# Attention ahead of the recurrence in both mixers of a two-layer trunk, with the fourth adaptive matrix loaded into other cells

## The chip, the cores and the metric

One NeuronCore of one Trainium2 chip runs the whole program in one launch. The metric is the device time of that launch in microseconds (us). The kernel is written in Bass: each engine (TensorE, VectorE, ScalarE, GpSimd) and each DMA queue has a program of its own that runs strictly in order, and semaphores are all that ties them together. In the profile PE is TensorE, PEld its weight loads, DVE VectorE, ACT ScalarE, POOL GpSimd; SPq is the queue of DMA transfers that SyncE issues, POOLq the one that GpSimd issues.

## What is computed

x is 256 tokens of 1024 channels in float32. Two layers, each a mixer and a channel mixer, each of the two behind its own adaptive modulation: four adaptive matrices in all (1024 rows by 3072 columns, three 1024-column parts: shift, scale, gate), numbered ada 0 to ada 3. The channel mixer of layer 0 is a dense SwiGLU, that of layer 1 routes over eight experts.

```python
def _modulate(c_act, w, b):
    m = (c_act @ w + b)[:, None, :]
    return jnp.split(m, 3, axis=-1)          # shift, scale, gate

def _hybrid_mixer(h, ...):
    c_q, c_kv, k_r, x_rec, g_rec = jnp.split(h @ w_in, IN_SPLITS, axis=-1)
    q = (_rms(c_q) @ w_q_up)                  # 8 heads of 64 + 32 (rope)
    kv = (_rms(c_kv) @ w_kv_up)               # 8 heads of 64 keys + 64 values
    attn = causal_attention(qf, kf, v)        # 2 blocks of 128 queries
    xr = causal_conv(x_rec, conv_w, conv_b)   # 4 taps
    r, i = sigmoid(xr @ w_a + b_a), sigmoid(xr @ w_x + b_x)   # block-diagonal
    log_a = 8 * r * log_sigmoid(lam)
    u = sqrt(-expm1(2 * log_a)) * (i * xr)
    h = scan(a=exp(log_a), u)                 # h[t] = a[t] * h[t-1] + u[t]
    rec = h * gelu(g_rec)
    return concat(_rms(attn), _rms(rec)) @ w_out

for l in range(2):                            # x = residual stream
    x += gate * _hybrid_mixer(_rms(x) * (1 + scale) + shift, ...)   # ada 0, ada 2
    x += gate * (_swiglu if l == 0 else _moe)(modulated _rms(x))    # ada 1, ada 3
```

## The kernel before

**The stages**, by the trace, in us from the start of the span: conditioning, ada 0 and layer 0's input projection (0 to 74); mixer 0 (74 to 162); the dense feed-forward (162 to 361); layer 1's input projection (ending at 406); mixer 1 (to 493); the router (to 507); the eight experts (to 1516). x stays in SBUF.

**Memory.** Weights stream from HBM through numbered cells of an arena (cells 0 to 2 of 3072 columns, 5 and up in the working area, `TOKENS` and 12 in other tensors). `fills` in `trunk()` is a table written out by hand: (what, which, piece, cell, waits). SyncE runs it from top to bottom; an entry with a wait holds all that stand behind it. The queue of layer 1's start is this: the last feed-forward pieces, the four pieces of w_in of layer 1, gate bias 2, ada 3's eight pieces of 128 rows (1.57 MB each), the small weights (q and kv up-projections, the block-diagonal gates), w_out, then the experts. The matrix of ada 2 goes through GpSimd's queue (the table `late`).

**An adaptive matrix** is summed over its 1024 rows by VectorE: `steps("ada", a, ks)` runs L1334 (one multiply by a column of c, piece 0) or L1336 (multiply and add to an accumulator, pieces 1 to 7), 3072 columns each; every piece is thus one step of the counter `ada_step`. TensorE then adds the 128 partitions (`ada_columns`) and VectorE forms the columns of shift and scale (`modulation(a)`, counter `mod`). In layer 1 ada 3's steps run while TensorE does the input projection (L643, L650), whose last column tiles are those of the latents and of the convolution.

**A mixer** (`mixer(l)` in each engine's program, the numbered lines are those of before):

- TensorE: transposes of the normed latents (L675), kv and q up-projections (L693), transposes of q and k per token block (`turn_qk`, L702), the scores of block 0 (L714, L720); then, ahead of the second block, the gate products of the recurrence `gates(0)`; transposes of q and k of block 1, its scores (L742, L745); `gates(1)`; transposes of the first block's probabilities s0 (L755), its outputs (L760), transposes and outputs of the second block's two halves of heads (L767, L776), transposes of the head outputs (L785), and the output projection (L795 in two parts, the attention's rows and then the recurrence's).
- VectorE: latents' scaling (L1522), taps of the convolution (`tap0` comes from ScalarE, taps 1 to 3 here), `heads(0)`, the two operations of GELU's polynomial (L1594, L1595), `heads(1)`, row maxima, the parts of the recurrence that don't need its gates, copies of transposed probabilities out of PSUM, reciprocals and head outputs, scans (in two parts around the copy of the transposed outputs), the products that end the recurrence, and `update`: x += gate * projection (L1652, L1654), with steps of ada 1 between in layer 0.
- ScalarE: root of norms, GELU's tanh, `gate_tanh(0)` (sigmoids as tanh), the exponentials of the decay (L1173, L1177), then `exps(0)`, `gate_tanh(1)`, the copy of s0's transposes, `exps(1)`, `exps(2)`, one more copy, the square root of the recurrence, squares for the norms.

Three of these hand-offs, as they stand in the code:

```python
pe.wait_ge(sem("xr"), l + 1)       # TensorE, ahead of block 1's transposes
gates(0)
turn_qk(1)
...
pe.wait_ge(sem("rg"), 2 * l + 1)   # TensorE, behind block 1's scores
gates(1)
pe.wait_ge(sem("p"), 3 * l + 1)    # then s0's transposes
```

The expert gate's bias (a single row) is issued by SyncE between the fourth and fifth piece of the experts, behind a wait for `ada_red` 4; VectorE adds it (L1674) before the router.

## Time and profile before

| | us |
|---|---|
| median of three runs | 1517.56 (1515.83 to 1518.67) |
| the profiled execution, its own time | 1520.06 |
| its span (first to last instruction) | 1518.3 |
| TensorE busy | 1457.4 (96% of the span) |
| VectorE busy | 1264.4 (83%) |
| ScalarE busy | 914.3 (60%) |
| DMA, mean rate | 309 GB/s |

The median is 2.5 us under the profiled execution; durations below come from that execution, and differences are taken against it. Busy shares are means over stages of unlike limits, so each stage is read on its own: from the chain of waits, from the timeline of one engine in a stretch (start, duration, and in brackets how long the engine had been idle and what released it), and from stretches in which each engine's busy time stands beside the length. The granted clock is 1.00 where TensorE runs at 2.4 GHz and 0.50 at 1.2 GHz; in between, both occurred in the stretch.

### The profile page before, as it was taken

To read this page: it belongs to the slowest core of one execution; us is meant where nothing else is said; L and a number is where in the kernel's file an instruction comes from. 1 tells how busy PE (TensorE), PEld (TensorE's weight loads), DVE (VectorE), ACT (ScalarE), POOL (GpSimd) and SP (SyncE) were. 2 spreads that over 40 slices of the span, in tenths; PEclk is the share of its full clock that TensorE was granted. 3 is DMA by queue.
4 is the path that set the end of the run, shared out by engine and by line. 5 is a ranking of instruction groups with operands and counts; after the bars stand their busy time and mean duration, and the time that the engine had idled before them with its cause. 6 is when DMAs were issued, how large, how long until landed. Compare 5 with 4: busy or idle time off the path is not lost.

```text
span 1518.3 us, 18807 instructions
## 1 busy us (share of the span) xinstructions
PE 1457.4 (96%) x7173; PEld 1192.0 (79%) x7173; DVE 1264.4 (83%) x1065; ACT 914.3 (60%) x812; POOL 13.8 (1%) x54
## 2 busy tenths in 40 slices
PE   4988899998889999999999999999999999999998
PEld 1765799996665888888888888888888888888886
DVE  3487678774776799899899999989989989999997
ACT  2072534442162677777677767767767767776774
POOL 1000000000000000000000000000000000000000
PEclk9998999999999899999999999999999999999999
DMA  9846469765837499999899899989989989999990
GB/s 353 334 194 227 164 224 376 270 242 216 321 111 259 143 363 372 337 349 380 330 354 378 322 359 378 376 322 363 374 329 351 376 333 357 361 335 368 365 351 28
DMA packets 191260, 468.68 MB, mean 309 GB/s; under 512 B 8471, under 2 KB 31221, under 8 KB 187126
## 3 DMA queue, kind: packets, MB, share of 16 engines
q1 hardware_dynamic: 186738, 451.17, 80.7%
q0 software_dynamic: 2256, 16.78, 2.7%
q8 instruction: 25, 0.41, 0.1%
q10 hardware_dynamic: 2228, 0.22, 0.1%
q14 instruction: 13, 0.11, 0.0%
HBM read 467.10 MB, written 1.05 MB: 308 GB/s over the span
## 4 chain that ended last, share of the span: by engine, by line
PE 82%; DVE 7%; ACT 4%; DMA 4%; SPq 2%; issue 1%; ACTq 0%; DVEq 0%
PE ps L960 20%; PE ps L962 20%; PE ps L961 20%; DMA arena<-in_w_ada 3%; PE ps L828 2%; PE ps L829 2%; PE ps L830 2%; PE ps L919 2%; PE ps L795 2%; DVE tokens L1336 2%; PE ps L999 2%; PE ps L837 1%; PE ps L838 1%; PE ps L836 1%; DMA tokens<-in_b_ada 1%
## 5 line engine op out<-in xcount | busy, mean ns | idle before, releaser
L1818 DVE TENSOR_TENSOR split_r<-arena,split_r 128x2048 fp32r<-128x2048 f32 x339 | 770.6, 2289 | 59.7 <-ACT split_r L1263 58.5
L1263 ACT ACTIVATE split_r<-arena 128x2048 fp32r<-128x2048 f32 x338 | 648.8, 1922 | 118.4 <-PE ps L962 118.3
L960 PE MATMUL ps<-split_r,tokens_r 128*128 128x512 f32 x1280 | 504.2, 394 | 0.2 <-DVE split_r L1818 0.2
L962 PE MATMUL ps<-split_r,tokens_r 128*128 128x512 f32 x1280 | 499.1, 390 | 0.0
L961 PE MATMUL ps<-split_r,tokens_r 128*128 128x512 f32 x1280 | 498.7, 390 | 0.0
L962 PEld LDWEIGHTS ps<-split_r,tokens_r 128*128 128x128 f32 x1280 | 240.2, 188 | 50.6
L960 PEld LDWEIGHTS ps<-split_r,tokens_r 128*128 128x128 f32 x1280 | 240.4, 188 | 49.1 <-DVE split_r L1818 0.6
L961 PEld LDWEIGHTS ps<-split_r,tokens_r 128*128 128x128 f32 x1280 | 240.5, 188 | 48.3
L828 PE MATMUL ps<-tokens_r,split_r 128*128 128x256 f32 x352 | 99.9, 284 | 5.3 <-DVE hT_r L1704 5.2
L829 PE MATMUL ps<-hT_r,split_r 128*128 128x256 f32 x352 | 100.1, 284 | 0.0
L830 PE MATMUL ps<-tokens_r,split_r 128*128 128x256 f32 x352 | 100.0, 284 | 0.0
L1696 DVE TENSOR_TENSOR split_r<-arena,split_r 128x2048 fp32r<-128x2048 f32 x33 | 75.3, 2292 | 20.1 <-ACT split_r L1220 19.1
L1220 ACT ACTIVATE split_r<-arena 128x2048 fp32r<-128x2048 f32 x33 | 63.0, 1915 | 43.9 <-PE ps L830 35.9
L828 PEld LDWEIGHTS ps<-tokens_r,split_r 128*128 128x128 f32 x352 | 67.6, 192 | 6.3 <-issue 5.4
L1286 ACT ACTIVATE F<-ps 128x512 f32<-128x512 f32 x56 | 33.6, 600 | 56.8 <-PE ps L962 56.8
L829 PEld LDWEIGHTS ps<-hT_r,split_r 128*128 128x128 f32 x352 | 67.3, 191 | 0.4
L830 PEld LDWEIGHTS ps<-tokens_r,split_r 128*128 128x128 f32 x352 | 67.4, 191 | 0.0
L1289 ACT ACTIVATE tokens_r<-ps 128x512 fp32r<-128x512 f32 x48 | 28.8, 600 | 59.1 <-PE ps L999 59.1
L795 PE MATMUL ps<-split,hT 128*128 128x512 f32 x128 | 58.9, 620 | 1.1 <-DVE hT L1640 1.1
L1102 ACT ACTIVATE arena<-arena 128x256 f32<-128x256 f32 (+2 forms) x12 | 3.6, 305 | 78.2 <-DVE arena L1522 78.2
L795 PEld LDWEIGHTS ps<-split,hT 128*128 128x128 f32 x128 | 25.1, 199 | 32.1 <-issue 32.1
L1336 DVE SCALAR_TENSOR_TENSOR tokens<-arena,cact,tokens 128x2048 f32<-128x2048 f32 (+1 forms) x11 | 31.2, 2837 | 12.8 <-DMA arena<-in_w_ada 12.3
(318 smaller groups left out, 1436.8 us busy)
## 6 DMA issues: line engine op xcount, KB each, us to landing
arena<-in_moe_w_gate SPq DMA_DIRECT2D x57, 2048.0 KB, 9.7
arena<-in_moe_w_up SPq DMA_DIRECT2D x57, 2048.0 KB, 9.4
arena<-in_moe_w_down SPq DMA_DIRECT2D x56, 2048.0 KB, 9.2
arena<-in_w_ada POOLq DMA_DIRECT2D x10, 1536.0 KB, 11.0
arena<-in_w_ada SPq DMA_DIRECT2D x14, 1024.0 KB, 12.7
arena<-in_ffn_w_gate SPq DMA_DIRECT2D x11, 1024.0 KB, 5.6
arena<-in_ffn_w_up SPq DMA_DIRECT2D x11, 1024.0 KB, 12.1
arena<-in_ffn_w_down SPq DMA_DIRECT2D x11, 1024.0 KB, 14.7
```

Of the source, the lines that this page charges most:

```text
L795: last = mm(ps[:, bank, :], mT[:, k, t * P:(t + 1) * P], parts[k // 3][:, k % 3, half * 512:(half + 1) * 512], start=(k == k0), stop=(k == ...
L828: mm(out_, h, xh, start=first, stop=False, skip_group_check=True)
L829: mm(out_, h, xl, start=False, stop=False, skip_group_check=True)
L830: return mm(out_, lo, xh, start=False, stop=last_, skip_group_check=True)
L960: mm(out_, xh, h, start=first, stop=False, skip_group_check=True)
L961: mm(out_, xh, lo, start=False, stop=False, skip_group_check=True)
L962: return mm(out_, xl, h, start=False, stop=last_, skip_group_check=True)
L1220: A(wh[:, n % SPLITS, :], unit(kind, c), ACT.Copy).then_inc(sem("f_hi"), 1)
L1263: A(wh[:, j % SPLITS, :], piece_half(j), ACT.Copy).then_inc(sem("w_hi"), 1)
L1336: ins = v.scalar_tensor_tensor(out=acc, in0=w, scalar=cact[:, k:k + 1], in1=acc, op0=ALU.mult, op1=ALU.add)
L1696: v.tensor_tensor(wl[:, n % SPLITS, :], unit(*units[n]), wh[:, n % SPLITS, :].bitcast(F32), ALU.subtract).then_inc(sem("f_lo"), 1)
L1818: v.tensor_tensor(wl[:, j % SPLITS, :], piece_half(j), wh[:, j % SPLITS, :].bitcast(F32), ALU.subtract).then_inc(sem("w_lo"), 1)
```

## The change

**Loads.** Pieces 0 and 1 of ada 3 go to cells 3 and 4 as soon as VectorE has split the down matrix of the feed-forward's last chunk but one (`f_lo` of unit d 9), ahead of gate bias 2; pieces 2 to 6 go to cells 12, 9, 5, 6 and 10 without further waits, piece 7 to cell 0. The accumulator stays where it was (`place((0, TOKENS, 0, TOKENS)[a])`). The zeroing of the block-diagonal tiles on GpSimd waits for ada 3's step 1, and the first two thirds of w_out for its steps 3 and 6. The expert gate's bias row leaves SyncE's table and is issued by GpSimd.

```diff
@@ fills @@
             ("win", 1, 0, 1, [("ada_step", step["ada", 2, 7])]),
+            ("ada", 3, 0, 3, [("f_lo", units.index(("d", 9)) + 1)]),
+            ("ada", 3, 1, 4, []),
             ("bias", 2, 0, None, [("f_wused", 3 * CHUNKS)]),
-            ("ada", 3, 0, TOKENS, []),
             ("ada", 3, 2, 12, []),
-            ("ada", 3, 3, 5, []),
-            ("ada", 3, 4, 6, []),
-            ("ada", 3, 1, 0, [("grow_ps", 3)]),
+            ("ada", 3, 3, 9, []),
+            ("ada", 3, 4, 5, []),
+            ("ada", 3, 5, 6, []),
+            ("ada", 3, 6, 10, []),
+            ("ada", 3, 7, 0, [("grow_ps", 3)]),
             ("small", 1, 0, None, [("wbd_zero", 2)]),
-            ("ada", 3, 5, 0, [("ada_step", step["ada", 3, 1])]),
-            ("ada", 3, 6, 12, [("ada_step", step["ada", 3, 2])]),
-            ("ada", 3, 7, 5, [("ada_step", step["ada", 3, 3])]),
...
@@ GpSimd @@
                 if l:
-                    pool.wait_ge(sem("f_lo"), 3 * CHUNKS)
+                    pool.wait_ge(sem("ada_step"), step["ada", 3, 1])
...
+            pool.wait_ge(sem("ada_red"), 4)
+            g.dma_start(moe_gate_bias, b_ada[1, 1, 2 * D:].unsqueeze(0)).then_inc(sem("late_bias_in"), 16)
```

SyncE's queue at layer 1's start, before: (w_in 1, bias 2, ada 3, the small weights, the rest of ada 3, w_out 1)

```order
L449 DMA arena<-in_w_in 128x2x1440 [waits ada_step] x2
L446 DMA split<-in_b_ada 128x1024 [waits f_wused]
L439 DMA tokens<-in_w_ada 128x3072
L439 DMA split<-in_w_ada 128x3072
L439 DMA arena<-in_w_ada 128x3072 x2
L439 DMA arena<-in_w_ada 128x3072 [waits grow_ps]
L458 DMA arena<-in_w_q_up 128x2x768 [waits wbd_zero]
```

and now:

```order
L445 DMA arena<-in_w_in 128x2x1440 [waits ada_step] x2
L437 DMA arena<-in_w_ada 128x3072 [waits f_lo]
L437 DMA arena<-in_w_ada 128x3072
L442 DMA split<-in_b_ada 128x1024 [waits f_wused]
L437 DMA split<-in_w_ada 128x3072 x2
L437 DMA arena<-in_w_ada 128x3072 x2
L437 DMA split<-in_w_ada 128x3072
L437 DMA arena<-in_w_ada 128x3072 [waits grow_ps]
L454 DMA arena<-in_w_q_up 128x2x768 [waits wbd_zero]
```

Two pieces of ada 3 stand ahead of the wait for the last feed-forward matmul (`f_wused`), and all eight stand ahead of the small weights, where three stood behind them.

**The mixers.** On TensorE `gates(0)` stands behind both blocks' scores; the transposes of s0 and of both halves of s1 follow one another, then the outputs; `gates(1)` is split in two halves, one ahead of the outputs' transposes and one behind. On VectorE the last tap stands behind the copy of kT; the copy of s0's transposes is VectorE's now, and GELU's polynomial and the recurrence's operations stand behind the copies; the scans are together. On ScalarE all three `exps` stand ahead of `gate_tanh(0)`.

```diff
@@ TensorE, mixer @@
-                pe.wait_ge(sem("xr"), l + 1)
-                gates(0)
                 turn_qk(1)
...
-                pe.wait_ge(sem("rg"), 2 * l + 1)
-                gates(1)
+                pe.wait_ge(sem("xr"), l + 1)
+                gates(0, range(LT))
...
-                pe.wait_ge(sem("pT_a"), 2 * l + 1)
-                pe.wait_ge(sem("rg"), 2 * l + 2)
...
+                pe.wait_ge(sem("pT_d"), 3 * l + 2)
...
+                pe.wait_ge(sem("rg"), 2 * l + 1)
+                gates(1, range(LT // 2))
                 if l == 1:
-                    ada_columns(place(TOKENS, 3 * D), range(KD), 7, step["ada", 3, KD - 1])
+                    ada_columns(place(TOKENS, 3 * D), range(KD), 5, step["ada", 3, KD - 1])
                 pe.wait_ge(sem("o_sb"), 2 * l + 2)
...
                 last.then_inc(sem("onT_ps"), 1)
+                gates(1, range(LT // 2, LT))
...
@@ ScalarE, mixer @@
-                act.wait_ge(sem("g_arg"), l + 1)
-                A(lq, lq, ACT.Tanh, scale=GELU_B).then_inc(sem("g_tanh"), 1)
                 turned_q(1, 6)
...
+                exps(0, s0, 4, P, H, list(range(H)))
+                exps(1, s1, 6, SEQ, 0, list(range(0, 4)))
+                exps(2, s1, 0, SEQ, 0, list(range(4, 8)))
                 gate_tanh(0, la)
...
@@ VectorE, mixer @@
                 heads(0)
-                dve.wait_ge(sem("g_sq"), l + 1)
-                link(v.tensor_scalar(lq, lq, GELU_A, 1.0, ALU.mult, ALU.add))
-                v.tensor_tensor(lq, lq, gr, ALU.mult).then_inc(sem("g_arg"), 1)
                 heads(1)
...
+                taps((TAPS - 1,))
                 row_max(1, 6, 2, SEQ, 0)
                 row_max(2, 0, 2, SEQ, 4)
+                dve.wait_ge(sem("pT_ps"), 3 * l + 1)
+                v.tensor_copy(PT[:, 0, :, :].rearrange("p h n -> p (h n)"), bank2(4)).then_inc(sem("pT_d"), 1)
...
-                if l == 0:
-                    steps("ada", 1, (3,))
...
                 if l == 0:
-                    steps("ada", 1, (4,))
+                    steps("ada", 1, (3, 4))
```

In layer 0 ada 1's step 3 thus moves behind the recurrence, and the load that waits for it (ada 1 piece 7) with it, and all loads behind that one in SyncE's queue. In layer 1 `modulation(3)` stands ahead of the recurrence's last part instead of behind it.

TensorE in a mixer, from block 1's scores to the projection, before (L714 are the gates here, L755 and L760 transposes and outputs of block 0, L767 and L776 those of block 1, L785 the transposes of the outputs):

```order
L745 MATMUL ps<-arena,hT 128x256 x2
L714 MATMUL ps<-arena 128x256 x4
L755 MATMUL ps<-ident,arena 128x128 x8
L760 MATMUL ps<-arena 128x64 x8
L767 MATMUL ps<-ident,arena 128x128 x16
L776 MATMUL ps<-arena 128x64 x16
L785 MATMUL ps<-ident,F 128x128 x8
L795 MATMUL ps<-split,hT 128x512 x16
```

and now (L712 are the gates, the rest in the same roles):

```order
L742 MATMUL ps<-arena,hT 128x256 x2
L712 MATMUL ps<-arena 128x256 x4
L752 MATMUL ps<-ident,arena 128x128 x8
L758 MATMUL ps<-ident,arena 128x128 x16
L763 MATMUL ps<-arena 128x64 x8
L772 MATMUL ps<-arena 128x64 x16
L712 MATMUL ps<-arena 128x256 x2
L783 MATMUL ps<-ident,F 128x128 x8
L712 MATMUL ps<-arena 128x256 x2
L794 MATMUL ps<-split,hT 128x512 x16
```

The gates of the recurrence that stood ahead of s0's transposes are the first set now, and the second set stands around the outputs' transposes.

ScalarE in a mixer, before (L1150 is GELU's tanh, L1156 the gates' tanh, L1173 and L1177 the decay, L1165 the exponentials of the scores, L1182 and L1186 copies):

```order
L1150 ACT_TABLE_LOAD
L1150 ACTIVATE arena<-arena 128x1024
L1137 ACTIVATE hT<-ps,gainc 96x8x128
L1156 ACTIVATE arena<-ps,hb 128x256 x4
L1173 ACTIVATE arena<-arena,nm 128x256 x4
L1177 ACTIVATE arena<-arena,m2ls 128x256 x4
L1165 ACTIVATE arena,den<-ps,mx 128x128 x8
L1156 ACTIVATE arena<-ps,hb 128x256 x4
L1182 ACTIVATE arena<-ps 128x1024
L1165 ACTIVATE arena,den<-ps,mx 128x256 x8
L1186 ACTIVATE arena<-ps 128x512
```

and now (L1136 is the copy of q's transposes, L1162 the exponentials, L1153 the gates, L1171 a copy, L1175 and L1179 the decay, L1182 GELU's tanh):

```order
L1136 ACTIVATE hT<-ps,gainc 96x8x128
L1162 ACT_TABLE_LOAD
L1162 ACTIVATE arena,den<-ps,mx 128x128 x8
L1162 ACTIVATE arena,den<-ps,mx 128x256 x8
L1153 ACTIVATE arena<-ps,hb 128x256 x4
L1171 ACTIVATE arena<-ps 128x512
L1175 ACTIVATE arena<-arena,nm 128x256 x4
L1179 ACTIVATE arena<-arena,m2ls 128x256 x4
L1182 ACTIVATE arena<-arena 128x1024
```

The exponentials stand ahead of all that the recurrence needs, with the load of the table directly ahead of them, and the copy of 1024 columns is gone from this engine.

## Rows read from the trace of the kernel before

**Rows 1.** The page, part 4: the chain that ended last, by engine.

```profile
PE 82%; DVE 7%; ACT 4%; DMA 4%; SPq 2%; issue 1%; ACTq 0%; DVEq 0%
```

**Rows 2.** A stretch: length, busy us of PE, PEld, DVE, ACT, POOL, clock, DMA share, GB/s.

```profile
507.00:1518.00 1011.00, 1004.47 (x4670) 833.22 (x4670) 923.28 (x600) 722.18 (x493) 0.00 (x0) 1.00 0.92 339
```

**Rows 3.** Timeline of DVE in layer 1: start, us, what, idle before it.

```profile
372.60 1.81 DVE L1334 TENSOR_SCALAR tokens<-tokens,cact 128x3072 f32<-128x3072 f32 x1
386.20 3.42 DVE L1336 SCALAR_TENSOR_TENSOR tokens<-arena,cact,tokens 128x3072 f32<-128x3072 f32 x1 [11.79 <-DMA arena<-in_w_ada]
...
410.38 1.09 DVE L1522 COPY arena<-ps 128x416 f32<-128x416 f32 x2
...
427.78 0.68 DVE L1594 TENSOR_SCALAR arena<-arena 128x1024 f32<-128x1024 f32 x1
428.50 1.22 DVE L1595 TENSOR_TENSOR arena<-arena,F 128x1024 f32<-128x1024 f32 x1
...
464.09 1.22 DVE L1645 SCALAR_TENSOR_TENSOR arena<-arena,F 128x1024 f32<-128x1024 f32 x1
```

**Rows 4.** Timeline of SP's DMA issues, 320 to 412 us.

```profile
321.30 20.63 SPq L449 DMA_DIRECT2D arena<-in_w_in  x4
...
363.01 4.86 SPq L439 DMA_DIRECT2D arena<-in_w_ada  x3
```

**Rows 5.** Stretches before and after the last feed-forward matmul.

```profile
342.00:361.60 19.60, 19.60 (x112) 16.25 (x110) 8.25 (x12) 3.36 (x5) 0.00 (x0) 1.00 0.22 76
361.60:389.00 27.40, 22.25 (x95) 16.44 (x95) 12.73 (x28) 5.78 (x14) 1.13 (x4) 1.00 0.95 363
```

**Rows 6.** Timeline of PE in layer 1.

```profile
411.53 1.54 PE L675 MATMUL ps<-ident,arena 128*128 128x128 f32 x6 [4.98 <-DVE arena L1522]
...
418.54 2.74 PE L693 MATMUL ps<-arena,F 128*128 128x384 f32 x8
...
438.75 0.36 PE L742 MATMUL ps<-F_r,identr 128*128 128x256 f32 x1 [1.40 <-DVE arena L1599]
...
460.87 1.09 PE L785 MATMUL ps<-ident,F 128*128 128x128 f32 x8 [0.17 <-DVE F L1628]
...
463.56 13.93 PE L795 MATMUL ps<-split,hT 128*128 128x512 f32 x32
```

**Rows 7.** Timeline of PE in layer 0.

```profile
76.28 0.82 PE L675 MATMUL ps<-ident,arena 128*128 128x128 f32 x6
...
80.39 2.74 PE L693 MATMUL ps<-arena,F 128*128 128x384 f32 x8
...
157.75 3.71 PE L577 MATMUL ps<-ones,tokens 128*128 128x96 f32 x32
```

**Rows 8.** Three stretches and their granted clock.

```profile
409.00:411.50 2.50, 0.00 (x0) 0.00 (x0) 2.44 (x3) 0.49 (x3) 0.00 (x0) 0.80 1.04 418
164.00:167.50 3.50, 0.00 (x0) 0.03 (x1) 3.46 (x7) 2.73 (x4) 0.00 (x0) 0.61 0.92 365
448.00:454.00 6.00, 5.67 (x27) 5.67 (x28) 0.95 (x2) 3.93 (x17) 0.00 (x0) 0.51 0.01 3
```

**Rows 9.** Stretch of layer 0, second scores to head outputs.

```profile
101.42:119.30 17.88, 14.53 (x100) 12.92 (x100) 14.81 (x16) 16.09 (x49) 0.00 (x0) 1.00 0.17 60
```

**Rows 10.** Stretch of layer 0, VectorE from the first heads to its last update but one.

```profile
84.84:155.12 70.28, 59.52 (x255) 37.86 (x254) 56.30 (x81) 32.28 (x79) 2.44 (x3) 0.93 0.64 229
```

**Rows 11.** Timeline of ACT and of DVE in layer 0.

```profile
83.17 0.81 ACT L1126 ACTIVATE arena<-ps 128x768 f32<-128x768 f32 x1 [0.47 <-PE ps L693]
...
84.84 0.75 DVE L1501 TENSOR_TENSOR arena<-ps,F 128x256 f32<-128x256 f32 x2
```

**Rows 12.** What DVE waited for, 83 to 161 us: total us, times, longest.

```profile
DVE F L1652 <- PE ps L795: 7.8, 6, 1.9
```

**Rows 13.** Timeline of ACT in layer 1.

```profile
433.37 1.28 ACT L1150 ACT_TABLE_LOAD   x1
```

**Rows 14.** DMA issues from 120 to 170 us: KB each, us to landing.

```profile
arena<-in_b_ada POOLq DMA_DIRECT2D x1, 4.0 KB, 9.3
```

144 lines of the change are left out of this document (71 added, 73 removed).

## The prediction

> **What bounds the kernel now.** I read the chain of waits first. TensorE holds 82% of it and VectorE 7% [rows 1]. Then the stretch of the experts: TensorE is busy 1004.47 of 1011.00 us at full clock, with DMA at 0.92 [rows 2]. Nothing in the diff touches that stage, so it only moves: whatever the change gives must show as an earlier start of the experts. The feed-forward is of the same kind (19.60 of 19.60 us busy in its last part, [rows 5]). What is left to gain lies in the two mixers and in front of them, and I went through those by the engines' timelines.
>
> In layer 1, TensorE ends the input projection and then stands 4.98 us until VectorE's L1522 [rows 6]. L1522 starts at 410.38, late, because VectorE comes from ada 3's eight steps: step 0 starts at 372.60 and takes 1.81, and then VectorE idles 11.79 us for the piece of step 1 [rows 3]. SyncE's queue tells why: w_in was issued by 341.93 (321.30 and 20.63), yet ada 3 only from about 363 [rows 4]. Between 342 and 361.6 the DMA engines were 0.22 busy, and from 361.6 to 389 they were full, 0.95 at 363 GB/s [rows 5]. So the first cause is when the transfers start, and the remedy has idle bandwidth to use.
>
> The same gap costs a second time. The granted clock is 0.80 in the idle stretch [rows 8], and from L675 to L693 TensorE takes 7.01 us (411.53 to 418.54) [rows 6], where layer 0 takes 4.11 (76.28 to 80.39) [rows 7].
>
> **The change part by part, layer 1.**
>
> *Transfers of ada 3.* Pieces 0 and 1 (1.57 MB each, 8.7 us at 363 GB/s) fit in the slack before 361.6. Behind it come gate bias 2 (0.52 MB) and six pieces, 9.96 MB, 27.4 us at 363 GB/s: the last lands near 389. The steps need one piece per 3.42 us: 372.60 + 1.81 + 7 x 3.42 = 398.4 for their end, the third piece at 377.8 (it lands at 367.5, after 2.09 MB) and the last at 395.0. No step waits. The small weights (another 1.57 MB) land near 394 and are wanted after L675, at 406 at the earliest. L1522 then waits for the projection's own last latents, not for the steps, and L675 follows the last projection matmul at 406.55: **-5.0**.
>
> *Clock.* Without the gap L675 to L693 runs as in layer 0, 4.1 instead of 7.0: **-2.9**.
>
> *GELU's polynomial* (0.68 and 1.22, [rows 3]) goes from between the two `heads` to where VectorE waits for TensorE anyway, so block 1's scores come **1.9** earlier. What covers it behind the copies is the wait for probabilities; without that cover it would cost 1.9 again.
>
> *Order on TensorE.* From block 1's scores (438.75) to the outputs' transposes (460.87) layer 1 takes 22.12 us [rows 6], part of it at half clock (0.51 from 448 to 454, [rows 8]) and in waits for the recurrence's tanh. Layer 0 shows that the same stretch holds 14.53 us of TensorE work at full clock [rows 9]. New in it: the four products of `gates(0)` replace those of `gates(1)`, half of `gates(1)` comes on top (0.9), half of ada 3's column sums lies in it (1.9, estimated from its share of the 22.12), and I leave 0.8 for waits at hand-offs: 18.1, so **-4.0**. The other half of `gates(1)` stands behind the transposes: **+0.9**.
>
> *Recurrence.* It now ends later relative to the attention. The projection's first half covers it: 13.93 us [rows 6] from about 450.7 to 464.6. VectorE has about ten full-width operations left after the transposes at 446.9 (1.22 each, [rows 3]), 12 us, and a few waits on ScalarE: it ends between 460 and 462. No cost; the cover is 3 us thick.
>
> *Expert gate's bias.* SyncE's wait between two pieces of the experts goes; nothing on the path waited for it: 0. The row now takes GpSimd's queue. There such a row (4 KB) landed 9.3 us after its issue [rows 14]; issued near 451 it lands at 460, and VectorE wants it near 469. The Trainium skill ("SBUF — State Buffer", section "SBUF: two separate sides") speaks against this: while VectorE copies float32 inside SBUF in its two-port mode, GpSimd cannot write descriptors, and a transfer of its queue starves. By that rule the row would land later by VectorE's copies at most; the 9.3 us above were measured beside a VectorE that was as busy.
>
> *ScalarE's order.* The load of the function table, 1.28 us [rows 13], stands directly ahead of the exponentials now. It is done while VectorE forms the row maxima, so 0. The Trainium skill ("ScalarE: Activation LUTs", section "What ACT_TABLE_LOAD costs") adds a drain of 1.38 us to each load; the row shows 1.28 us. By the page the sum would be about 0.5 us higher in each layer.
>
> Layer 1: -5.0 -2.9 -1.9 -4.0 +0.9 = **-12.9**. The bounds: if the scores' stretch keeps its clock and waits (-0 for -4.0) it is -8.9; if the 0.8 of waits and the 0.9 behind the transposes turn out to be hidden, -14.6.
>
> **Layer 0.** The same order, but VectorE also has ada 1's steps there, and becomes the one that ends last. In its stretch from 84.84 to 155.12 (70.28 us) it is busy 56.30 and idle 13.98 [rows 10]; 7.8 of the idle time are six waits of L1652 for the projection [rows 12], which TensorE's earlier end removes. Changes: it may start at 83.98, when ScalarE's copy of the latents' projections (83.17 + 0.81) ends, instead of 84.84 [rows 11]: -0.9. The last tap (four operations, 1.2 to 1.7 us by L1645's 1.22 for as many columns; I take 1.7) and s0's copy (1024 columns, 1.2) come in: +2.9. Idle: 13.98 - 7.8 + 1.4 (it now waits for s0's transposes): 7.6. So 83.98 + 56.3 + 2.9 + 7.6 = 150.8 instead of 155.1: -4.3 at most. That is not all kept. TensorE, ahead now, idles about 5 us before the norm's transposes and L577 (157.75, [rows 7]), and a gap of 4.98 us is what preceded the fall of the clock in layer 1 [rows 6, 8]; the clock was also 0.61 from 164 to 167.5 [rows 8]. At half clock the first 4 to 6 us of work take 2 to 3.3 more (layer 1's 2.9 is the nearest row; I take 2.8). Layer 0: **-1.5**, between -0.5 and -4.6.
>
> *The displaced step.* ada 1's step 3 moves behind the recurrence; the piece that waits for it is issued some 16 us later (about thirteen operations of 1.22 us, [rows 3], now stand ahead of the step), and with it the first feed-forward pieces behind it in SyncE's queue. Those are wanted only behind the projection, from 155 on, and a MB takes under 3 us at 363 GB/s [rows 5]; by my count the step ends near 130, 20 us of cover are left. 0.
>
> **Sum:** -12.9 -1.5 = -14.4, 1520.06 - 14.4 = 1505.7 for an execution like the profiled one; the median of the runs is 2.5 us under it, so **1503.2 us**. The difference that a measurement of this kernel tells from none is 0.2%, 3 us.
>
> **Rivals.**
>
> 1. *The transfers stay late* (8%). If SyncE reaches ada 3 only with the last feed-forward matmul (a cell that is not free, a wait in front of it), the 5.0 and 2.9 stay: -6.5, **1511**. For it: SyncE's queue is in order and today issued nothing between 341.93 and 363 [rows 4]. Against: the new first wait stands ahead of `f_wused`. "The change doesn't do what it says" is this case or the next, with 3% for no difference at all.
>
> 2. *The recurrence's tail becomes the bound* (14%). ScalarE has everything of the recurrence behind 16 exponentials now, and VectorE its products behind the head outputs. If ScalarE is 3 us later than I count, the cover of 3 us is gone and the second half of the projection waits 2 to 4 us in layer 1: **1505 to 1507**.
>
> 3. *Slower* (5%): *the clock*. The projection of layer 1 is two halves of 13.93 us [rows 6] at full clock. If the order leaves TensorE in short work with gaps before it, as it was from 448 to 454 at 0.51 [rows 8], and it stays at 1.2 GHz through both halves, they cost 27.9 us more: 1503.2 + 27.9 = **1531**. It decides against the change once 14.4 us of full-clock work runs at half clock. Against it: before, the low stretch at 448 was followed by both halves at full clock.
>
> 4. *Layer 0's clock does not fall*: 1500.4, a variant of the forecast and in its range.
>
> **How the numbers follow.** Forecast 70%, rivals 8, 14 and 5, no difference 3. The range takes in layer 0 from -0.5 to -4.6, layer 1 from -14.6 to -8.9, and rival 2: **1497.5 to 1509.5**; rival 1 and rival 3 lie outside. Faster by over 0.2%: 70 + 14 + 8 = 0.92; same 0.03; slower 0.05.
>
> **What would show it.** In the profile after: ada 3's first two issues before 361 and no idle time over 1 us ahead of any L1336 in layer 1; the latents' transposes near 406.5 with the up-projections 4.1 us behind; 18 us from block 1's scores to the outputs' transposes; the projection's two halves without a gap between them; experts starting near 493 instead of 507; in layer 0 no waits of the update for the projection, and TensorE idle for some 5 us before L577 at half clock behind. Wrong would be: a wait of TensorE for the recurrence between the halves, or an idle VectorE in ada 3.

## The result, and the profile after

| | before | changed |
|---|---|---|
| median | 1518.12 us (1515.83 to 1520.01, 4 runs) | 1506.50 us (1501.89 to 1507.64, 4 runs) |
| ratio, 95% interval | | 0.9918 [0.9893, 0.9943] |
| profiled execution, its own time | 1520.06 | 1506.64 |
| its span | 1518.3 | 1504.9 |

The change makes the kernel 11.6 us faster by the medians, 13.4 us by the two profiled executions. The forecast was 1503.2 us, 14.4 under the median then known; the result is 3.3 us above it, inside its range. To see where the time went, I cut each trace at the same instructions of TensorE and took differences of their starts. a is the first transpose of the latents in layer 0, b the last feed-forward matmul, c the latents' transposes of layer 1, d the scores of block 1, e the start of the output projection, f the router's first transposes, g the experts' first matmul.

```
us            start-a   a-b     b-c    c-d    d-e    e-f    f-g    g-end
before         76.28   284.97  50.28  27.22  24.81  29.88  20.55  1004.31
changed        76.72   283.03  45.56  22.53  20.81  29.50  22.54  1004.21
difference     +0.44    -1.94  -4.72  -4.69  -4.00  -0.38  +1.99    -0.10
foreseen        0       -1.5   -5.0   -4.8   -3.1    0      0       0
```

In the chain of waits, by engine, what is not TensorE's fell from 18% to 10% [rows 1]:

```profile
PE 90%; DVE 6%; ACT 2%; issue 1%; DMA 1%; ACTq 0%; DVEq 0%
```

SyncE's queue, changed kernel, 340 to 412 us: two pieces of ada 3 are issued 19 us ahead of the gate bias, where all stood behind it [rows 4].

```profile
340.86 0.81 SPq L437 DMA_DIRECT2D arena<-in_w_ada  x2
360.17 0.33 SPq L442 DMA_DIRECT2D split<-in_b_ada  x1
```

Stretches of the changed kernel: first VectorE's of layer 0 [rows 10], then two of [rows 8] and the two of [rows 5] (length, busy us of PE, PEld, DVE, ACT, POOL, clock, DMA share, GB/s):

```profile
84.07:151.00 66.93, 58.64 (x261) 37.04 (x259) 58.99 (x86) 31.88 (x79) 2.44 (x3) 1.00 0.56 207
...
409.00:411.50 2.50, 2.50 (x10) 1.65 (x9) 2.46 (x7) 1.85 (x2) 0.00 (x0) 1.00 0.30 41
...
448.00:454.00 6.00, 6.00 (x21) 3.13 (x20) 5.04 (x6) 4.23 (x8) 0.50 (x1) 1.00 0.02 5
342.00:361.60 19.60, 18.14 (x99) 14.74 (x97) 7.09 (x13) 4.84 (x7) 0.00 (x0) 1.00 0.57 234
361.60:389.00 27.40, 24.55 (x99) 18.27 (x100) 25.17 (x30) 4.30 (x12) 1.13 (x4) 0.94 1.01 406
```

DMA is busy 0.57 instead of 0.22 from 342 to 361.6. At 409 to 411.5 and 448 to 454 TensorE works where it stood or ran at half clock, and the clock is 1.00. In layer 0's stretch it is 1.00 too, where it was 0.93. VectorE's last update but one there ends at 150.9, and the prediction counted 150.8 (busy 58.99 us, counted 59.2; idle 7.94, counted 7.6).

VectorE in layer 1 [rows 3]: no step waits for a piece, the last ends at 397.5 (394.10 + 3.42), and VectorE now waits for the latents, not they for it. The last row is the addition of the expert gate's bias.

```profile
394.10 3.42 DVE L1332 SCALAR_TENSOR_TENSOR tokens<-arena,cact,tokens 128x3072 f32<-128x3072 f32 x1
400.73 0.59 DVE L1518 COPY arena<-ps 128x416 f32<-128x416 f32 x1 [3.21 <-PE ps L641]
...
466.21 1.21 DVE L1671 TENSOR_TENSOR tokens<-tokens 1x1024 f32<-1x1024 f32 x1
```

TensorE in layer 1 [rows 6], first up to the up-projections, then from block 1's scores on; nothing stands between the projection's matmuls (L648, one group ends at 405.5) and the transposes, and the two halves of the output projection follow each other.

```profile
405.31 0.82 PE L673 MATMUL ps<-ident,arena 128*128 128x128 f32 x6
...
409.42 2.74 PE L691 MATMUL ps<-arena,F 128*128 128x384 f32 x8
```

```profile
427.84 0.36 PE L739 MATMUL ps<-F_r,identr 128*128 128x256 f32 x1 [1.41 <-DVE arena L1596]
...
445.16 1.04 PE L783 MATMUL ps<-ident,F 128*128 128x128 f32 x8
...
448.65 13.93 PE L794 MATMUL ps<-split,hT 128*128 128x512 f32 x32
...
464.33 13.98 PE L794 MATMUL ps<-split,hT 128*128 128x512 f32 x32
```

TensorE in layer 0 [rows 7], one line of before, then the changed kernel: the gap of 4.95 us that the prediction spoke of, and behind it the column sums in 5.74 us instead of 3.71. Before, the clock had fallen earlier, in the projection: its first half took 17.02 us there (16.5 to 16.8 in the other three traces with layer 0's old order) and takes 13.97 now.

```profile
124.50 17.02 PE L795 MATMUL ps<-split,hT 128*128 128x512 f32 x32 [1.13 <-DVE hT L1640]
```

```profile
117.13 13.97 PE L794 MATMUL ps<-split,hT 128*128 128x512 f32 x32 [0.27 <-DVE hT L1627]
...
152.37 1.97 PE L588 MATMUL ps<-ident,F 128*128 128x128 f32 x8 [4.95 <-DVE F L1351]
154.13 5.74 PE L575 MATMUL ps<-ones,tokens 128*128 128x96 f32 x32
```

### The profile page after: what moved, and what is told of

Read it like the earlier page. It is cut to its first block, busy times and chain, and to the rows that moved or that the text cites. A ratio compares the mean times of both kernels' runs of the same rounds, so it can differ in the third digit from the quotient of the medians.

```text
span 1504.9 us, 18806 instructions
## 1 busy us (share of the span) xinstructions
PE 1450.9 (96%) x7173; PEld 1189.9 (79%) x7173; DVE 1267.0 (84%) x1067; ACT 912.6 (61%) x810; POOL 14.2 (1%) x55
## 3 DMA queue, kind: packets, MB, share of 16 engines
HBM read 467.10 MB, written 1.05 MB: 311 GB/s over the span
## 4 chain that ended last, share of the span: by engine, by line
PE 90%; DVE 6%; ACT 2%; issue 1%; DMA 1%; ACTq 0%; DVEq 0%
PE ps L959 20%; PE ps L961 20%; PE ps L960 20%; PE ps L648 4%; PE ps L827 2%; PE ps L828 2%; PE ps L829 2%; PE ps L918 2%; PE ps L794 2%; PE ps L641 2%; PE ps L998 2%; PE ps L836 1%; PE ps L837 1%; PE ps L835 1%; PE ps L575 1%
## 5 line engine op out<-in xcount | busy, mean ns | idle before, releaser
L1693 DVE TENSOR_TENSOR split_r<-arena,split_r 128x2048 fp32r<-128x2048 f32 x33 | 75.3, 2291 | 19.5 <-ACT split_r L1216 18.6
L1285 ACT ACTIVATE tokens_r<-ps 128x512 fp32r<-128x512 f32 x48 | 28.8, 599 | 59.2 <-PE ps L998 59.2
L1332 DVE SCALAR_TENSOR_TENSOR arena<-arena,cact 128x1024 f32<-128x1024 f32 (+1 forms) x20 | 40.6, 2029 | 0.4
```

What stands on the lines that cost most here:

```text
L1693: v.tensor_tensor(wl[:, n % SPLITS, :], unit(*units[n]), wh[:, n % SPLITS, :].bitcast(F32), ALU.subtract).then_inc(sem("f_lo"), 1)
```

## The experiments

Medians, with the kernel before on the same chip beside each. The first four were run on one chip, the next four on another, the last four on a third.

| run | median us | before | ratio [95%] | a-b | b-c | c-d | d-e | e-f | f-g |
|---|---|---|---|---|---|---|---|---|---|
| loads only | 1511.84 | 1518.55 | 0.9956 [0.9943, 0.9969] | 285.97 | 45.37 | 25.03 | 23.31 | 30.08 | 18.59 |
| order only | 1510.90 | 1518.55 | 0.9948 [0.9936, 0.9961] | 282.06 | 50.47 | 25.22 | 20.81 | 29.49 | 20.91 |
| layer 1 only | 1503.45 | 1518.55 | 0.9897 [0.9884, 0.9910] | 285.04 | 45.66 | 22.54 | 20.81 | 29.49 | 20.91 |
| pair late | 1503.76 | 1518.55 | 0.9910 [0.9896, 0.9924] | 282.68 | 45.28 | 22.54 | 20.81 | 29.49 | 20.71 |
| changed again | 1505.68 | 1519.29 | 0.9907 [0.9887, 0.9928] | 282.46 | 45.99 | 22.53 | 20.81 | 29.50 | 20.91 |
| steps in waits | 1500.96 | 1519.29 | 0.9885 [0.9865, 0.9904] | 281.94 | 46.00 | 22.53 | 20.81 | 29.49 | 19.12 |
| filled, long | 1505.45 | 1519.29 | 0.9907 [0.9887, 0.9927] | 282.66 | 45.39 | 22.54 | 20.80 | 29.50 | 20.60 |
| polynomial back | 1506.19 | 1519.29 | 0.9921 [0.9900, 0.9942] | 286.40 | 45.13 | 24.41 | 20.80 | 29.49 | 19.04 |
| filled, short | 1497.74 | 1519.04 | 0.9862 [0.9842, 0.9882] | 279.50 | 45.26 | 22.54 | 20.81 | 29.49 | 20.65 |
| step and filling | 1497.17 | 1519.04 | 0.9857 [0.9837, 0.9877] | 277.93 | 45.13 | 22.54 | 20.81 | 29.49 | 20.62 |
| before, filled | 1519.63 | 1519.04 | 1.0014 [0.9999, 1.0029] | 285.44 | 50.32 | 26.64 | 23.51 | 30.07 | 18.92 |
| bias on SyncE | 1513.19 | 1519.04 | 0.9970 [0.9957, 0.9983] | 282.86 | 45.14 | 22.54 | 20.80 | 38.98 | 21.28 |

The stages c to f repeat within 0.1 us between traces of the same code; a to b and b to c move by about 1 us, f to g by 2 and the end by 3 (the experts take 1002.1 or up to 1005.6 us). So a few tenths of a microsecond can be read from c to f, and no single total can be read that finely. A kernel with one trace only (loads only, order only, before filled) rests on that one.

### Loads only, order only

The first is the kernel before with the new entries of `fills` for ada 3 and w_out and GpSimd's new wait (the first diff of the section on the change, without the bias row). The second is the changed kernel with the old entries, and so on GpSimd:

```diff
-                    pool.wait_ge(sem("ada_step"), step["ada", 3, 1])
+                    pool.wait_ge(sem("f_lo"), 3 * CHUNKS)
```

> The kernel before with nothing changed but the loads of ada 3 (cells, places in the queue, the wait of GpSimd and of w_out). My theory has two terms for it, 5.0 us for the steps' wait and 2.9 us for the clock behind the gap: 7.9 us faster than before, the latents' transposes directly behind the projection and the up-projections 4.1 us behind them. The rival: the earlier end is used up by the mixer's own waits (block 1's scores still wait for VectorE and the recurrence), so that 5 us or less are left at the output projection and under 5 at the end.

> The changed kernel with the loads of ada 3 as before (the same cells, waits and places as in the kernel before). By my sum the order alone gives 1.9 and 4.0 less 0.9 in layer 1 and 1.1 to 1.5 in layer 0: 6 to 6.5 us faster than before, and 7 to 8 slower than the changed kernel. If the two parts overlap (the order only helps once the projection's end is early), it gives less than 4 us; if the order is what removed the clock's fall behind the gap, it gives 9 or more.

Measured: 6.7 us (loads, where 7.9 were expected) and 7.7 (order, where 6 to 6.5 were). The two ratios multiplied are 0.9904, and the changed kernel had 0.9918 and 0.9907 on other chips. The two parts add up, as far as the totals can tell. The loads give 4.9 at b to c, and the order gives nothing there. But the loads do not give 2.9 more at c to d: they give 2.2 (27.22 to 25.03), and the order gives 2.5 on top instead of 1.9 (to 22.53). Taken the other way round, the order alone gives 2.0 (to 25.22) and the loads 2.7 on top. TensorE with the loads alone:

```profile
407.84 0.82 PE L675 MATMUL ps<-ident,arena 128*128 128x128 f32 x6
...
411.95 2.74 PE L693 MATMUL ps<-arena,F 128*128 128x384 f32 x8
...
432.87 0.36 PE L742 MATMUL ps<-F_r,identr 128*128 128x256 f32 x1 [1.40 <-DVE arena L1599]
```

The up-projections stand 4.11 us behind the transposes, as foreseen, and yet the scores come only 2.2 us earlier. More than TensorE's clock sets their time.

### Is it the clock? The kernel before with its gap filled

```diff
                     if i == 3:
                         last.then_inc(sem("rec_ps"), 1)
+                        if l == 1:
+                            for _ in range(20):
+                                mm(ps[:, 3, 0:P], ident[:, :], ident[:, :], start=True, stop=True)
                         pe.wait_ge(sem("cn"), 2 * l + 2)
```

> The kernel before with 20 filling matmuls in the 4.98 us that TensorE waits for the latents in layer 1, and nothing else: the wait stays, only the clock's share is taken out. By my term the up-projections come 4.1 instead of 7.0 us behind the latents' transposes: 2.9 us earlier, and 2.9 us less at layer 1's output projection. If the clock falls there for another reason, or the mixer's waits for VectorE take up what TensorE gains (VectorE is the releaser of most of its waits there), it is 0 to 1.5.

TensorE, and VectorE beside it, in the filled kernel:

```profile
412.40 0.88 PE L678 MATMUL ps<-ident,arena 128*128 128x128 f32 x6 [0.16 <-DVE arena L1525]
...
416.56 2.77 PE L696 MATMUL ps<-arena,F 128*128 128x384 f32 x8
...
439.04 0.35 PE L745 MATMUL ps<-F_r,identr 128*128 128x256 f32 x1 [1.41 <-DVE arena L1602]
```

```profile
417.43 5.09 DVE L1552 SCALAR_TENSOR_TENSOR arena<-F,colA,arena 128x256 f32<-128x256 f32 x12 [1.00 <-ACT arena L1115]
422.44 0.75 DVE L1504 TENSOR_TENSOR arena<-ps,F 128x256 f32<-128x256 f32 x2
```

The clock's 2.9 us are there (416.56 - 412.40 = 4.16 instead of 7.01), and the scores come 26.64 us behind the transposes instead of 27.22: 0.6 is left. VectorE runs from its taps (417.43) into the heads without a wait. The slow up-projections had cost it one wait of 0.5 us. Behind the scores another 1.3 us are saved (d to e 23.51). The median shows none of this (1.0014 [0.9999, 1.0029]); the profiled execution, 1516.0 us, was the fastest of twelve. So of the 2.2 us that the loads give at c to d with the old order, 0.6 is clock; the other 1.6 is VectorE's lead: with the loads early it has scaled, rotated and normalised the latents before TensorE comes to their transposes, and the taps start 3.43 us behind these (411.27, trace of the loads alone) instead of 5.04 (416.57).

With the new order the split is another. VectorE in the trace of the order alone, and in the changed kernel; L1125 is ScalarE's copy of the first up-projections:

```profile
420.15 0.76 DVE L1497 TENSOR_TENSOR arena<-ps,F 128x256 f32<-128x256 f32 x2 [2.06 <-ACT arena L1125]
```

```profile
413.11 0.76 DVE L1497 TENSOR_TENSOR arena<-ps,F 128x256 f32<-128x256 f32 x2 [0.99 <-ACT arena L1125]
```

The last tap no longer stands ahead of the heads, so VectorE gets there sooner (at 418.09) and waits 2.06 us for the late up-projections (6.79 us behind the transposes, clock 0.63 from 409.7 to 417). Had they come 4.11 us behind, the copy would have been done before VectorE needed it. So by my estimate 2.1 of the 2.7 us that the loads give there are clock and 0.6 is VectorE's lead. What a faster TensorE gives the scores is 0.6 us in one order and about 2.1 in the other; no run fills the gap with the new order.

### GELU's polynomial back between the heads

```diff
                 heads(0)
+                dve.wait_ge(sem("g_sq"), l + 1)
+                link(v.tensor_scalar(lq, lq, GELU_A, 1.0, ALU.mult, ALU.add))
+                v.tensor_tensor(lq, lq, gr, ALU.mult).then_inc(sem("g_arg"), 1)
                 heads(1)
```

> The changed kernel with GELU's two polynomial operations between the two heads, as before. By my term the scores of block 1 come 1.9 us later in layer 1 and so does the output projection: 1.9 us slower than the changed kernel there; in layer 0, where VectorE is the bound and the operations only change place on it, 0 to 0.7 us. If VectorE waits for block 1's q and k anyway, it costs nothing in either layer.

In layer 1 c to d is 24.41 instead of 22.53: 1.88 us, the term to a tenth. In layer 0 it costs at least as much: the first feed-forward matmul comes 91.03 us behind a instead of 88.4 to 89.1, and a to b is 286.40 instead of 282.1 to 283.0. The median (1506.19) does not tell the two kernels apart. I had called VectorE the bound there, and an operation that only changes place on it free. But VectorE still has waits in that stretch, and an operation that fills one is free only in the wait.

### Ada 3's first pieces behind the gate bias

```diff
-            ("ada", 3, 0, 3, [("f_lo", units.index(("d", 9)) + 1)]),
-            ("ada", 3, 1, 4, []),
             ("bias", 2, 0, None, [("f_wused", 3 * CHUNKS)]),
+            ("ada", 3, 0, 3, []),
+            ("ada", 3, 1, 4, []),
```

> The changed kernel with ada 3's pieces 0 and 1 behind the gate bias, so that SyncE issues none of the eight before the last feed-forward matmul. If the order of the queue alone is what matters (no small weights and no step's wait between the eight), 13.1 MB at 363 to 406 GB/s end at 394 to 398, the last step at 398 to 401 and VectorE is still in time for the latents at 400.7: within 1 us of the changed kernel. If the idle bandwidth before 361 is what gives the gain, the steps wait for their pieces and 3 to 5 us of the 5.0 come back.

b to c is 45.28: the same. VectorE, in the same trace:

```profile
380.18 3.42 DVE L1332 SCALAR_TENSOR_TENSOR tokens<-split,cact,tokens 128x3072 f32<-128x3072 f32 x1 [1.13 <-DMA split<-in_w_ada]
...
394.96 3.42 DVE L1332 SCALAR_TENSOR_TENSOR tokens<-arena,cact,tokens 128x3072 f32<-128x3072 f32 x1 [0.29 <-DMA arena<-in_w_ada]
399.54 0.59 DVE L1518 COPY arena<-ps 128x416 f32<-128x416 f32 x1 [1.16 <-PE ps L641]
```

From step 3 on each step waits some 0.3 us for its piece, 1.1 at the first, and the latents still make VectorE wait 1.16. So the idle bandwidth before 361, from which I argued, is not what gives the 5 us. What is left as the cause is the order of the queue. Before, the piece of step 1 stood fifth of ada 3's, behind a wait, and three pieces stood behind the small weights; VectorE stood 11.79 us for that fifth one [rows 3]. Which of these two counts for more no run separates.

### Layer 0 in its old order

Each engine's mixer has both orders here, the old for layer 0; on TensorE:

```diff
+                if l == 0:
+                    def gates(g):
...
+                    pe.wait_ge(sem("xr"), l + 1)
+                    gates(0)
+                    turn_qk(1)
...
+                else:
+                    def gates(g, tiles):
```

> The changed kernel with layer 0's mixer in the order of before on TensorE, VectorE and ScalarE, ada 1's step 3 in its old place too. If layer 0's new order gives only what the trace shows at the first feed-forward matmul and after it (1.1 to 1.8 us), this is 1 to 2 us slower than the changed kernel. If the low clock behind the new gap of 4.95 us eats all of it, it is the same within 0.5 us; if VectorE as the bound costs more than it gives, it is faster.

1503.45 us, ratio 0.9897, and 0.9907 for the changed kernel on another chip: no difference that the runs can show. In the traces layer 0's old order takes 285.0 to 286.0 us from a to b (four traces), the new one 282.1 to 283.0 (five): 2 to 3 us, of which nothing can be seen in the totals of these two. So layer 0's gain stands in the traces only; the kernel with the old order there has, if anything, the lower median.

### The clock in layer 0, and the gap that VectorE leaves

Matmuls whose results nobody reads, behind the output projection of layer 0 and behind the transposes of the second norm (34 and 34 in the first run, then 20 and 12, then 13 and 12 together with a moved step):

```diff
+                if l == 0:
+                    for _ in range(34):
+                        mm(ps[:, 4, 0:P], ident[:, :], ident[:, :], start=True, stop=True)
...
+                for _ in range(34):
+                    mm(ps[:, 3, 0:P], ident[:, :], ident[:, :], start=True, stop=True)
```

> The changed kernel with 34 additional 128 x 128 matmuls of no use in each of TensorE's two gaps of layer 0 (ahead of the norm's transposes of the feed-forward, and ahead of its first matmul), written to banks that nobody reads. If the gap is what brings the clock down, as I put it, L575 runs at full clock behind it (3.7 us instead of 5.74) and so do the first feed-forward matmuls (13 of them took 0.21 instead of 0.12): the feed-forward is 2.5 to 3.5 us earlier than in the changed kernel. If the clock comes down whatever TensorE does there, the filling matmuls at half clock last longer than the gaps and it is 0 to 2 us later.

```profile
147.15 7.75 PE L820 MATMUL ps<-ident 128*128 128x128 f32 x68
...
155.61 3.71 PE L575 MATMUL ps<-ones,tokens 128*128 128x96 f32 x32
```

The clock stays at 1.00 from 144 to 172 and the column sums take 3.71 us. But 34 such matmuls last 7.75 us (68 rows of 0.114, since a float32 matmul makes two), longer than the gap. The feed-forward's start is 1.8 to 2.0 us later, and its end the same (a to b 282.66).

> As the filled kernel before, with 20 and 12 matmuls instead of 34 and 34 (0.228 us each, so 4.6 us in the gap of 4.95 and 2.7 in the second, whose first part VectorE needs in any case). With the clock kept, L575 takes 3.7 instead of 5.8 us, the second transposes come 2 us earlier, and all feed-forward matmuls run at full clock from the first: relative to the latents' transposes of layer 0 the first feed-forward matmul is 2.5 to 3 us earlier than in the changed kernel and 1.3 more are saved behind it, 3.5 to 4 us in all at the feed-forward's end. If something else than TensorE (VectorE's chain behind the second norm) sets that start, it is 1.3 to 2.

```profile
147.07 4.63 PE L820 MATMUL ps<-ident 128*128 128x128 f32 x40
...
153.11 3.71 PE L575 MATMUL ps<-ones,tokens 128*128 128x96 f32 x32
156.65 1.04 PE L588 MATMUL ps<-ident,F 128*128 128x128 f32 x8
```

```profile
164.00:168.00 4.00, 4.00 (x23) 4.00 (x22) 3.82 (x2) 1.95 (x2) 0.00 (x0) 0.58 1.09 361
```

Now a gap of 0.48 us is left and the second norm's transposes come at 156.65 instead of 159.70. The feed-forward starts at full clock, but not for long: a second gap of 2.28 us stands before it (162.65), and from 164 to 168 the clock is 0.58. So not every loss is gone; only the longer filling kept the clock up throughout. a to b is 279.50, 3.0 us less than the changed kernel's 282.46 and 283.03. The median is 1497.74 us, 21.3 under before. Of the 8 us to the changed kernel's 1505.68 (another chip), the trace explains 3.0 here; 3.4 lie in the experts' stretch (1002.13 against 1005.56), told of below. That stretch took 1002.1 or 1002.2 us in five other traces too, four of them without this filling, so those 3.4 are not put down to it.

> The changed kernel with ada 1's step 3 placed ahead of VectorE's copy of s0's transposes and step 4 ahead of the second block's outputs, where VectorE waits 1.2 and 1.8 us in layer 0 (and a wait for the squares of o in SyncE's queue, ahead of the second chunk's loads, in place of the order that step 4 gave). If VectorE is the bound of layer 0, as I say, its last update ends 3 us earlier, TensorE's gap of 4.95 us shrinks to about 2.5 and the first feed-forward matmul comes 2.5 to 3 us earlier than in the changed kernel. If TensorE or the order of attention is the bound there, the steps delay it and nothing is gained or up to 3 us are lost.

```diff
+                if l == 0:
+                    steps("ada", 1, (3,))
                 dve.wait_ge(sem("pT_ps"), 3 * l + 1)
...
+                if l == 0:
+                    steps("ada", 1, (4,))
                 heads_out(1)
```

```profile
109.35 2.77 PE L763 MATMUL ps<-arena 128*128 128x64 f32 x16 [1.58 <-DVE arena L1606]
111.91 7.04 PE L772 MATMUL ps<-arena 128*128 128x64 f32 x32
```

```profile
108.00:112.00 4.00, 2.65 (x17) 2.65 (x17) 3.93 (x6) 4.00 (x10) 0.00 (x0) 0.80 0.69 248
112.00:116.00 4.00, 4.00 (x21) 4.00 (x20) 3.69 (x4) 1.42 (x2) 0.00 (x0) 0.50 0.00 0
```

The first outputs wait 1.58 us for VectorE's copies, the clock falls (0.80, then 0.50), and the second block's outputs take 7.04 us instead of 3.74. The output projection of layer 0 starts at 123.97 instead of 117.13, and VectorE's last update ends later, not 3 us earlier. That is the expectation's second case. It is not slower all the same (a to b 281.94): the projection ends later, so that TensorE does not stand before the transposes, and the column sums are at full clock. The loss and the gain cancel. The median is 4.7 us under the changed kernel's on the same chip all the same; in the two traces 1.8 us of it lie in the router and 3.4 in the experts' stretch, and why these moved stays open.

> The changed kernel with one step only (ada 1's step 3) in VectorE's wait of 1.8 us ahead of the second block's outputs, step 4 left where it is, and 13 and 12 filling matmuls. The step absorbs the wait, so VectorE's last update ends 1.5 to 1.8 us earlier, and the clock is kept: 5 to 5.8 us earlier at the feed-forward's end than the changed kernel, 1500 to 1501 us where the changed kernel has 1505.5. If a delay of the outputs' transposes (0.6 us) is enough to bring down the clock in the projection, as two steps in the waits did from 112 us on, TensorE's projection lasts 2 to 3 us more, and what is gained is the filling alone, 3 to 4.

```profile
112.95 2.35 DVE L1338 SCALAR_TENSOR_TENSOR tokens<-arena,cact,tokens 128x2048 f32<-128x2048 f32 x1
115.34 0.69 DVE L1622 TENSOR_TENSOR F<-ps,den 128x512 f32<-128x512 f32 x1
```

One step (2.35 us) in the wait of 1.8 us: the outputs follow it at once. Counted from a, the output projection starts 0.6 us later than in the changed kernel, the transposes behind it 1.75 earlier (151.17 - 77.27 against 152.37 - 76.72), and a to b is 277.93: 1.6 less than with the filling alone, 4.5 to 5.1 less than the changed kernel. The median, 1497.17 us (ratio 0.9857 [0.9837, 0.9877]), is the best of all; against the filling alone (1497.74) the runs do not tell them apart.

### The bias row in SyncE's queue

```diff
             fills.append(("moe", 0, i, None, ...
+            if i == 4:
+                fills.append(("bias", 3, 0, None, [("ada_red", 4)]))
```

> The changed kernel with the expert gate's bias row back in SyncE's queue, between the experts' fifth and sixth piece, behind its wait for ada 3's sums. By my reading nothing on the path waits for it: the same time as the changed kernel within 0.5 us at the experts' start, though VectorE may wait up to 4 us for it. If SyncE's wait holds back the experts' fifth piece, or VectorE's wait delays the updates, the router or the first expert starts 1 to 4 us later.

SyncE, VectorE and TensorE in that trace:

```profile
459.14 2.95 SPq L419 DMA_DIRECT2D arena<-in_moe_w_down  x1
462.14 0.51 SPq L444 DMA_DIRECT2D tokens<-in_b_ada  x1
```

```profile
476.13 1.21 DVE L1673 TENSOR_TENSOR tokens<-tokens 1x1024 f32<-1x1024 f32 x1 [11.49 <-DMA tokens<-in_b_ada]
```

```profile
477.47 5.12 PE L796 MATMUL ps<-split,hT 128*128 128x512 f32 x8 [4.13 <-DVE st L1342]
486.10 1.09 PE L610 MATMUL ps<-ident,F 128*128 128x128 f32 x8 [3.50 <-DVE F L1353]
```

This is the surprise of the study. It is the row's old place (behind the experts' fifth piece; the text above says between the fourth and the fifth). SyncE's queue comes to the row only at 462.14, behind three transfers of 2 MB, and VectorE stands 11.49 us for it. All its updates of the second half and the root behind it are queued there, so TensorE stands 4.13 us before its last eight matmuls of the projection (that wait releases them) and 3.50 us before the router's transposes. e to f is 38.98 instead of 29.5, and the kernel is at 0.9970 where the changed kernel was at 0.9907. In GpSimd's queue the row is issued at 449.11, 13 us sooner, and takes 2.3 us from issue to landing:

```profile
tokens<-in_b_ada POOLq DMA_DIRECT2D x1, 4.0 KB, 2.3
```

Two things differ here, and no run separates them: the place in a queue, and what else the DMA engines carry. They were idle (share 0.02 from 448 to 454) when the changed kernel's row went. Beside full DMA engines (share 1.05 from 150 to 165 us, kernel before) the row of [rows 14] took 9.3 us in GpSimd's queue.

In the kernel before, VectorE waited 4.4 us for that row, off the path. The loads alone did not change this (e to f 30.08, a wait of 4.6). The new order does. Before, VectorE's updates of the attention half waited for the projection (2 us each) and VectorE came to the addition at 479. Now the projection's first half is nearly through when the recurrence ends, the updates run in one go from 460.16, and VectorE is at the addition at 466.21.

### The same kernel again

> The changed kernel itself, once more, on the chip of the next three. If the spread of the first result (1501.9 to 1507.6) lies in the router's clock, its experts start between 497 and 501 us and everything up to the end of the output projection of layer 1 stands within 1 us of the first profile; its median is 1503 to 1507, ratio 0.990 to 0.992.

1505.68 us, ratio 0.9907 [0.9887, 0.9928]; c to f repeats the first trace within 0.1 us. As far as the traces show, the spread (1502.4 to 1507.9) lies where TensorE's clock differs. One place is the router, another the last 15 us. In 5 us of them the changed kernel ran at half clock in this trace, and the filled one at full clock (length, busy us by engine, clock, DMA share, GB/s):

```profile
1495.10:1500.10 5.00, 5.00 (x7) 1.96 (x6) 2.92 (x4) 0.00 (x0) 0.00 (x0) 0.50 0.03 13
```

```profile
1486.90:1491.90 5.00, 2.64 (x6) 1.25 (x7) 5.00 (x5) 1.50 (x1) 0.00 (x0) 1.00 0.00 0
```

## Why the prediction was right, and where it was not

*The steps of ada 3 (-5.0).* -4.72, and 4.3 to 5.2 in the traces of the other kernels with the new loads. Right. The reason I gave for it was half right: the queue before was late, but starting early in idle bandwidth is not needed.

*The clock (-2.9) and the polynomial (-1.9).* Their sum, -4.8, stands against -4.69 measured. How it splits depends on which part comes first. With the order first it is 2.0 for the order and 2.7 for the loads, near the 1.9 and 2.9 of the sum. With the loads first it is 2.2 for the loads (clock 0.6, VectorE's lead 1.6) and 2.5 for the order (the polynomial 1.9; 0.6 is left, and VectorE reaches the heads that much sooner without the last tap, 7.80 against 8.44 us behind the transposes). The weak step is "without the gap L675 to L693 runs as in layer 0: -2.9". TensorE's own time fell by just that, but I took it for time on the path, without asking who is waited for behind it. The profile of before had the row: TensorE's wait ahead of the next transposes had VectorE as its releaser. That the term came out near 2.9 all the same is in part luck: VectorE's lead, which the sum has not, stands in for the part of the clock that never reached the scores.

*Order on TensorE (-4.0, +0.9).* d to e is -4.00 where I had -3.1, and the order alone gives all of it (20.81). To the outputs' transposes it is 17.32 us where I had 18.1, and the half of `gates(1)` behind them costs 0.8. At least 1.5 of the 4.0 is clock: it was 0.51 from 448 to 454, it is 1.00 now, and with the loads alone, where the old order takes 23.31, it stood between:

```profile
441.00:447.00 6.00, 4.73 (x29) 4.55 (x28) 2.06 (x3) 5.04 (x19) 0.00 (x0) 0.73 0.01 3
```

The other 2.5 are order and what was left of the low clock; no run parts them.

*Recurrence and the projection's halves (0).* Right: the recurrence's last product ends at 459.6, and the second half follows the sums at 464.33 with no wait. Rivals 1 and 2 did not come.

*Layer 0 (-1.5).* -1.94 in the profiled pair, 2.7 between the means of the traces. The mechanism is as put: VectorE ends last, TensorE idles 4.95 us (5 foreseen) and restarts at half clock. The filling shows that this clock costs 3 us. What I did not see is that before the clock fell too, inside the projection (17.02 us instead of 13.97): the new order gives back 3 us there and loses as much behind the gap. The displaced step of ada 1 cost nothing; it ended at 130.3, near 130 foreseen.

*The expert gate's bias (0).* Right as the effect of the change as a whole, wrong as a term. Its move keeps much of the rest: without it the changed kernel loses 9.5 us at e to f. I wrote "nothing on the path waited for it: 0", which was true of the order before. I checked the new queue against a use near 469 (it came at 466.21), and never asked what the old place would have cost in the new order. The Trainium skill ("SBUF — State Buffer", section "SBUF: two separate sides") warns of transfers in GpSimd's queue while VectorE copies float32 inside SBUF. Here the row landed in 2.3 us; VectorE's work in that time (from 449.15, L1633 and L1635) was no such copy, so this does not test the rule.

*The table load (0).* Right in size, but not for the reason given. The row maxima of block 0 end at 426.12, before the load starts, so they do not cover it; what does is ScalarE's wait for block 1's maxima. ScalarE in the changed kernel:

```profile
426.73 1.28 ACT L1162 ACT_TABLE_LOAD   x1
428.02 0.37 ACT L1162 ACTIVATE arena<-ps,mx 128x128 f32<-128x128 f32 x1
...
431.56 0.47 ACT L1162 ACTIVATE arena<-ps,mx 128x256 f32<-128x256 f32 x1 [0.63 <-DVE mx L1590]
```

The Trainium skill ("ScalarE: Activation LUTs", section "What ACT_TABLE_LOAD costs") adds a drain of 1.38 us to the load. The trace does not agree: the operation before the load ends at 426.71, the load itself at 428.01, and the first exponential starts at 428.02.

*The rest, 2 us.* f to g is 22.54 instead of 20.55: a stretch for which the sum has no term. TensorE in the router, before and after:

```profile
498.34 3.71 PE L874 MATMUL ps<-F,hT 128*128 128x8 f32 x32
```

```profile
483.41 4.57 PE L873 MATMUL ps<-F,hT 128*128 128x8 f32 x32
```

The logits take 4.57 us instead of 3.71, since the clock falls already in them. With the old order the router took 18.6 to 20.6 us (three traces), with the new one 20.6 to 22.5 in nine traces and 19.0 or 19.1 in two. So the new order tends to lose 1 to 2 us here, by an earlier fall of the clock. Why it falls earlier stays open; no run filled the router. This loss of 2.0 is what brings the profiled gain to 13.4; up to f the trace stood 15.7 us ahead less the 0.4 of its later a, more than my 14.4.

*The range.* Its terms give 1498.4 to 1508.2; the range adds about 1 us at each end without a reason. The result lies inside both.

*Slower, by a half clock through the projection (5%).* It did not come: the halves took 13.93 and 13.98 us. But its mechanism exists in small: in the run with two steps in the waits, a wait of 1.6 us was followed by a stretch at 0.50 and 6 us lost on TensorE up to the projection.

## What to carry to other kernels

A piece of a change that saves nothing in the old order can be what the new order stands on: price each part against the changed kernel too, by asking which wait sits in front of the work that has moved forward. A time saved on one engine is worth only what the next wait of the path leaves of it (2.9 us on TensorE were 0.6 in the old order and about 2.1, by estimate, in the new), and an engine called the bound still has waits that work can be put in. Where TensorE must stand for some 5 us before short work, useless matmuls that end just before it resumes kept its clock over that work and were worth 3 us; too many of them cost as much as they give.

## What the runs showed of the hardware

- In layer 0 of the changed kernel a gap of 4.95 us on TensorE was followed by a granted clock of one half of full (1.2 GHz; 0.50 from 152 to 156), and the work behind it took 2.9 us more (1.97 for 1.09 and 5.74 for 3.71). With matmuls in the gap the clock stayed at 1.00 (2.4 GHz) over that work in three kernels. In two of them it fell behind a later gap of 2.28 us (0.58 from 164 to 168 in one); in the third, with that gap filled too, it did not.
- A row of 4 KB took 2.3 us in GpSimd's queue with the DMA engines idle, 9.3 us there with them full, and about 14 us (462.14 to 476.1) in SyncE's queue behind three transfers of 2 MB.
- A table load of 1.28 us on ScalarE was followed by the next operation within 0.01 us.
- Executions of one kernel on one chip differed by 5.5 us (1502.4 to 1507.9, the changed kernel) and by 10 us (1511.6 to 1521.7, the kernel before, 23 executions). Their mean clock goes with it (0.989 and 0.984; 0.987 and 0.980).
